# Sparse attention of block 1: the multiply of the probabilities by their reciprocal sums, issued on GpSimd in place of VectorE

## The reference, cut to what matters

```python
y_a = conformer_conv(a_val, a_gate, ...)   # GLU, causal depthwise conv of 31 taps, LayerNorm, swish
y_b = short_gated_conv(b_gate, c_gate, b_h, sc_dw[l])
y_c = dsa_attention(q, k, v, q_idx, k_idx, w_idx)
x = x + jnp.concatenate([y_a, y_b, y_c], axis=-1) @ w_out[l]

# dsa_attention: 8 heads of 64; the top 128 keys of each query by an indexer's score, causal
s = jnp.einsum('bqhd,bqkhd->bqhk', qb, k_sel).astype(jnp.float32) * (dh ** -0.5)
s = jnp.where(jnp.isfinite(top_val)[:, :, None, :], s, -jnp.inf)
p = jax.nn.softmax(s, axis=-1).astype(v.dtype)
return jnp.einsum('bqhk,bqkhd->bqhd', p, v_sel)
```

## Time and profile before

| | |
|---|---|
| median of three runs | 3725.43 us |
| profiled execution | 3722.92 us |
| span of its instructions | 3721.0 us |
| TensorE busy | 97% of the span |
| VectorE busy | 54% |
| ScalarE busy | 33% |
| GpSimd busy | 15% |
| share of TensorE in the chain that ended last | 91% |
| first sparse attention (l = 0) | 550.3 to 612.6 us |
| second (l = 1) | 1741.7 to 1807.4 us |

### The profile page before, as it was taken

The page is one execution under the profiler, slowest core; times in us unless marked ns, Lnnn a source line. Parts: engine busy times, 40 slices in busy tenths (PEclk is TensorE's granted clock), DMA queues, the critical chain, the costliest instruction groups (busy, mean ns, idle before and its releaser), DMA issues.

```text
span 3721.0 us, 45399 instructions
## 1 busy us (share of the span) xinstructions
PE 3624.0 (97%) x15894; PEld 2840.8 (76%) x15894; DVE 2009.4 (54%) x3014; ACT 1210.5 (33%) x1783; POOL 552.4 (15%) x378
## 2 busy tenths in 40 slices
PE   8999998999999999998999999999999999899998
PEld 6887775877887888776687888776688877678887
DVE  5445796555445544679645444635644463564444
ACT  4223354332223222345433322323322232332222
POOL 0000382020002000236203000300300020030002
PEclk9999999999999999999999999999999999999999
DMA  5332331423333333332141333322133332113331
GB/s 149 96 94 80 97 85 41 124 63 94 93 96 91 94 93 96 87 87 68 57 133 53 92 91 96 95 69 63 46 95 92 96 91 80 57 51 96 94 92 62
DMA packets 617232, 318.93 MB, mean 86 GB/s; under 512 B 12144, under 2 KB 615176, under 8 KB 617096
## 3 DMA queue, kind: packets, MB, share of 16 engines
q1 hardware_dynamic: 617096, 317.15, 29.6%
HBM read 314.75 MB, written 2.10 MB: 85 GB/s over the span
## 4 chain that ended last, share of the span: by engine, by line
PE 91%; DVE 4%; ACT 2%; issue 1%; POOL 1%; DMA 0%; POOLq 0%; DVEq 0%; ACTq 0%; SPq 0%
PE bank L443 28%; PE bank L445 28%; PE bank L444 28%; PE bank L537 1%; PE bank L706 1%; PE bank L612 1%; PE bank L690 1%; PE bank L724 1%; PE bank L533 1%; DVE spare L1691 1%; PE bank L732 0%; PE bank L743 0%; DVE u_lo L1182 0%; DVE w_lo L1178 0%; POOL mem L1752 0%
## 5 line engine op out<-in xcount | busy, mean ns | idle before, releaser
L860 ACT ACTIVATE w_hi<-raw 128x1024 fp32r<-128x1024 f32 x602 | 638.1, 1060 | 1854.5 <-PE bank L445 1853.3
L443 PE MATMUL bank<-u_hi,w_hi 128*128 128x512 f32 x3024 | 1220.1, 403 | 2.5 <-DVE u_lo L1182 1.8
L445 PE MATMUL bank<-u_hi,w_lo 128*128 128x512 f32 x3024 | 1197.5, 396 | 0.0
L444 PE MATMUL bank<-u_lo,w_hi 128*128 128x512 f32 x3024 | 1193.6, 395 | 0.0
L1178 DVE TENSOR_TENSOR w_lo<-raw,w_hi 128x1024 fp32r<-128x1024 f32 x602 | 794.9, 1320 | 724.1 <-ACT w_hi L860 723.6
L443 PEld LDWEIGHTS bank<-u_hi,w_hi 128*128 128x128 f32 x3024 | 568.9, 188 | 156.2 <-issue 16.5
L444 PEld LDWEIGHTS bank<-u_lo,w_hi 128*128 128x128 f32 x3024 | 568.9, 188 | 143.4 <-issue 9.3
L445 PEld LDWEIGHTS bank<-u_hi,w_lo 128*128 128x128 f32 x3024 | 568.7, 188 | 139.6
L443 PE MATMUL bank<-h_hi,w_hi 128*128 128x512 f32 (+1 forms) x1696 | 646.2, 381 | 2.1 <-DVE h_lo L1182 2.1
L445 PE MATMUL bank<-h_hi,w_lo 128*128 128x512 f32 (+1 forms) x1696 | 641.6, 378 | 0.0
L444 PE MATMUL bank<-h_lo,w_hi 128*128 128x512 f32 (+1 forms) x1696 | 641.1, 378 | 0.0
(11 more groups left out here) (208 smaller groups left out, 2217.3 us busy)
## 6 DMA issues: line engine op xcount, KB each, us to landing
raw<-in_w_in SPq DMA_DIRECT2D x96, 512.0 KB, 3.8
raw<-in_ffn_w_gate SPq DMA_DIRECT2D x88, 512.0 KB, 3.8
raw<-in_ffn_w_up SPq DMA_DIRECT2D x88, 512.0 KB, 3.8
raw<-in_ffn_w_down SPq DMA_DIRECT2D x64, 512.0 KB, 3.9
raw<-in_w_gate SPq DMA_DIRECT2D x44, 512.0 KB, 3.8
raw<-in_w_up SPq DMA_DIRECT2D x44, 512.0 KB, 3.8
raw<-in_w_out SPq DMA_DIRECT2D x32, 512.0 KB, 4.0
raw<-in_xa_wkv SPq DMA_DIRECT2D x32, 512.0 KB, 3.9
```

The source lines that it names most:

```text
L443: mm(o, w_hi[:, s, w], rhs_hi[:, r], start=k == 0, stop=False)
L444: mm(o, w_hi[:, s, w], rhs_lo[:, r], start=False, stop=False)
L445: ins = mm(o, w_lo[:, s, w], rhs_hi[:, r], start=False, stop=k == kn - 1)
L860: a(w_hi[:, p.slot, :], raw[:, p.slot, :], ACT.Copy).then_inc(rounded, 1)
```

## The change

The reciprocal stays on VectorE, and releases a new semaphore `p_inv`. VectorE no longer waits for it, and goes on. GpSimd waits for `p_inv`, multiplies the two tiles and releases `p_norm`. Its squares for the LayerNorm now stand behind the multiplies of step 4, and its power behind those of step 6.

```diff
@@ block.vector, the sparse attention
                     if 1 <= i < 17:
-                        b, n = (i - 1) % 4, P * ((i - 1) % 4 + 1)
+                        b = (i - 1) % 4
                         v.wait_ge(p_exp, s0 + i)
-                        chain.done(v, nc.vector.reciprocal(small[:, 16 + 2 * b:18 + 2 * b], small[:, 8 + 2 * b:10 + 2 * b]))
-                        for e in range(2):
-                            p_ = pair_s[b][e][:, 0:n]
-                            ins = ts(p_, p_, row_inv[2 * b + e], None, ALU.mult)
-                        ins.then_inc(p_norm, 1)
+                        nc.vector.reciprocal(small[:, 16 + 2 * b:18 + 2 * b], small[:, 8 + 2 * b:10 + 2 * b]).then_inc(p_inv, 1)
@@ block.gpsimd, behind the taps
-                for c in range(2):
-                    pool.wait_ge(ln_cent, 2 * l + c + 1)
-                    tt(y_buf[c], conv[c], conv[c], ALU.mult).then_inc(ln_sq, 1)
-                pool.wait_ge(ln_v, l + 1)
-                tt(ln_inv, ln_var, minus_half[:, 0:NQ], ALU.pow).then_inc(ln_i, 1)
+                for i in range(16):
+                    b, n = i % 4, P * (i % 4 + 1)
+                    pool.wait_ge(p_inv, 16 * l + i + 1)
+                    for e in range(2):
+                        p_ = pair_s[b][e][:, 0:n]
+                        ins = ts(p_, p_, row_inv[2 * b + e], None, ALU.mult)
+                    ins.then_inc(p_norm, 1)
+                    if i == 4:
+                        for c in range(2):
+                            pool.wait_ge(ln_cent, 2 * l + c + 1)
+                            tt(y_buf[c], conv[c], conv[c], ALU.mult).then_inc(ln_sq, 1)
+                    if i == 6:
+                        pool.wait_ge(ln_v, l + 1)
+                        tt(ln_inv, ln_var, minus_half[:, 0:NQ], ALU.pow).then_inc(ln_i, 1)
```

More of the change, by code:

```diff
@@ L325, in two_blocks @@
         masked = sem("masked")
-        s_mm, s_min, p_exp, p_norm, t_mm, t_set, pv_mm = (
-            sem(n) for n in ("s_mm", "s_min", "p_exp", "p_norm", "t_mm", "t_set", "pv_mm"))
+        s_mm, s_min, p_exp, p_inv, p_norm, t_mm, t_set, pv_mm = (
+            sem(n) for n in ("s_mm", "s_min", "p_exp", "p_inv", "p_norm", "t_mm", "t_set", "pv_mm"))
         o_rounded, o_ready = sem("o_rounded"), sem("o_ready")
```

## The result

The changed kernel is slower: 3734.96 us, median of seven runs (3727.38 to 3738.38), against 3722.44 us for the kernel before in seven runs beside it. The ratio is 1.003, with a 95% interval of 1.0019 to 1.0041. That is 12.5 us, above the range of the prediction (3717 to 3730) and on the other side of its forecast. Its profiled execution took 3730.14 us with a span of 3727.9 us.

A forecast was written before the change was run, and what follows sets the result against it. TensorE, busy 97% of the span, was taken as the bound, so only VectorE multiplies it waits for counted. Gains of 1.30 and 0.53 us, 1.83 in each of two attentions, gave 3.7 us: 3721.8 us, range 3717 to 3730.

The forecast's parts named there:

- The price of one multiply: GpSimd's tensor_scalar multiply, absent from the trace, was estimated at 0.71 us for 512 columns.
- The upper end, 1.04: Range end for GpSimd's multiply at 512 columns, from the two-operand multiply; gain 1.11 us a block, 3723.2 us.
- Rival B: GpSimd's multiply costs 1.81 us, like its two-tensor additions; 2.35 us a block slower, 3730.1 us; chance 0.12.
- its line between 1.04 and 1.81 us: Gain or loss by GpSimd's multiply price at 512 columns; the sign turns at about 1.29 us.
- Rival C: TensorE's clock decides in the attentions, falling either way by 3.4 us: 3718.3 or 3725.1 us; chance 0.16.
- The tail: Step 15's multiplies before the last transposes: 1.47 us on GpSimd fits in 2.01; at 1.04 each, 0.12 is lost.
- some 1.4 us nearer to the start of the attention: Centring of the LayerNorm (L1512) on VectorE, expected this much earlier as a sign of being right.
- The first gain is 1.30 us: GpSimd's LayerNorm squares start at 573.26 in place of 574.56, behind the multiplies of step 4.
- TensorE's own work hides it: GpSimd's power behind step 6's pair costs nothing, since its diagonal is wanted only after the value product.
- The lock: Shared ports of VectorE and GpSimd: L1182 waits for GpSimd's multiply until 570.95, a gain of 0.97 instead of 1.41.
- rival D: Lock or GpSimd order takes the 0.97 gain down by 0.71: 3723.2 us, or 3725.4 with L1526's neighbours delayed; chance 0.12.
- small gain of step 9: Step 9's multiplies leave VectorE ahead of L1526, adding 0.53 us, less than ScalarE's wait of 0.76.

The follow-up runs named there:

- e2: Changed kernel with GpSimd's multiply written as a two-tensor form reading the reciprocals as a broadcast: 3719.55 us, 0.9992 of the kernel before.
- e11: Changed kernel with a constant 0.01 in place of the column of reciprocals, leaving out the division by row sums: 3728.75 us, one run.
- e3: Changed kernel with constant matmuls nobody reads ahead of TensorE's waits for the squares and the last multiply: 3722.86 us, 1.0002 of the kernel before.
- e1: Changed kernel without the multiplies, leaving out the division by the row sums: 3717.43 us, 0.9986 of the kernel before.
- e4: Changed kernel with the multiplies of steps 14 and 15 back on VectorE: 3726.29 us, 1.0014 of the kernel before.
- e10: Changed kernel with the multiplies of steps 0 to 4 back on VectorE: 3727.73 us, 1.0022 of the kernel before.
- e7: Changed kernel with e2's form, steps 2, 14 and 15 on VectorE, squares and power moved ahead as in e6: 3716.76 us, 0.9991 of the kernel before.
- e6: Changed kernel with the squares ahead of step 4's multiplies and the power ahead of step 6's: 3726.20 us, 1.0014 of the kernel before.
- e5: Changed kernel with only steps 5 to 13 multiplied on GpSimd, the others back on VectorE: 3719.85 us, 0.9997 of the kernel before.

## Why the prediction was wrong

**The price of one multiply is the step that failed.** "I take 0.71, since the instruction reads one tensor and is of the kind of the 281 ns row" put together the fixed part of one instruction and the slope of another. The fixed part was about right, the slope was not: a memset reads nothing, and its 0.84 ns a column says nothing of an instruction that does; the multiply has 2.5. (The prediction's 0.47 us for 128 columns "by that slope" lies on the line from the 281 ns row to the 1.04 us; the memset's slope would give 0.72. The change's row has 0.63 at 128 columns.) The upper end, 1.04, was taken from the two-operand multiply as if a second tensor could only make it dearer. e2 and e11 show the opposite: the form that reads one tensor and a constant takes 1.55, the one that reads two 1.14.

**Rival B was right in its place and its sign, at 0.12.** But the price alone does not carry the sum: its line between 1.04 and 1.81 us, taken at 1.58, gives +1.3 us a block, 2.6 of the 12.5 in all. By that line the squares come 0.65 us late and the tail loses 1.20 us; the sums of squares came 0.8 and 1.1 us late in the two blocks, and the last wait grew by 1.86 us. What is missing is a queue on GpSimd and the clock.

**The clock was the second step.** Rival C had it as luck, half each way, independent of the rest. But at the two places the waits and the clock go together: behind a wait of 1.4 and 2.6 us for the squares and of 2.2 us for the last pair, both blocks ran the next work at the low clock, and fillers in the same waits took it away there (e3). In the first block 2.7 us of waiting brought 5.6 us of slower work with it. The earlier trace rows held the hint, a value product of 4.10 us at 0.58, and the prediction itself remarked that TensorE "had often idled" before it; it used this for a spread, not for the price of a wait. Rival C is not refuted for the rest of the attention: the value products between the two places fall either way, and in the second block three of them together took 3.2 us less than before the change. The runs of one kernel differ with the clock as well: the 33 runs of the kernel before beside e1 to e4 go from 3716.03 us at a granted 0.985 to 3726.56 at 0.981.

**The tail** had "2.01 us, of which VectorE used 0.88" and asked whether 0.05 + 2 x price fit. It assumed that GpSimd is free when the last reciprocal comes. This row of VectorE over time in the kernel after has that reciprocal:

```profile
608.05 0.17 DVE L1483 RECIPROCAL small<-small 128x2 f32<-128x2 f32 x1 [0.98 <-ACT spare L1012]
```

GpSimd had begun the pair of step 14 at 606.57 and came to the last pair only at 609.38, as GpSimd over time shows:

```profile
609.38 3.10 POOL L1792 TENSOR_SCALAR spare<-spare,small 128x512 f32<-128x512 f32 x2
```

The last reciprocal was done at 608.22, so the last pair stood 1.2 us in a queue before its own 3.1 us. e10 puts the tail at 0.22%, e4 takes it away.

**The front.** The centring "some 1.4 us nearer to the start of the attention" held and more: it starts at 572.01, 21.4 us after the start of the attention against 23.5 before, 2.0 us earlier. "The first gain is 1.30 us" did not: the squares stood behind GpSimd's piece of 6.76 us and started 0.6 us late, the sums of squares 0.8. The prediction let GpSimd begin step 3 as soon as its reciprocal was there. But the pair of step 2, off the chain while VectorE did it, now stood ahead of it in GpSimd's order and ran from 568.69 to about 571.1, while the reciprocal of step 3 was done at 570.28. This is the same queue as in the tail. e1 shows the relief that the argument was about, 1.9 us, and e2 and e7 keep 1.4 to 1.6 of it. "TensorE's own work hides it", of the power, failed in the first block: the power came late at 587.28, and TensorE waited 0.71 us for the diagonal.

**The lock** was to make L1182 wait for GpSimd's multiply. It did not, as VectorE over time in the kernel after shows; GpSimd was multiplying without a break from 568.69 to 575.45:

```profile
570.63 0.69 DVE L1182 SCALAR_TENSOR_TENSOR h_lo<-mem,h_hi 128x512 fp32r<-128x512 f32 x1 [0.35 <-ACT h_hi L1020]
```

In e2, beside the two-tensor form, the same instruction is stretched:

```profile
571.44 1.31 DVE L1182 SCALAR_TENSOR_TENSOR h_lo<-mem,h_hi 128x512 fp32r<-128x512 f32 x1 [0.35 <-ACT h_hi L1020]
```

So the half of rival D that had L1182 wait for whole pairs of multiplies is out: in the change they block it not at all. The other half, the order on GpSimd, was there: the squares waited for three whole pairs, and e6 gets about half of the loss back by the order.

**Right** were the small gain of step 9 (TensorE's wait ahead of its transposes fell from 2.56 to 1.90 us in both blocks) and the reading that only the work ahead of the squares, ahead of L1526 and in the tail counts: e5, which leaves the first and the last alone, changes nothing that can be told.

**What stays open.** The median less the two attentions of the profiled execution is 3591 to 3597 us for all these kernels but e1, where it is 3603.5: its profiled execution, at 3710.41 us, is one of its three fastest, and the attentions of the others may have been longer. Each kernel has one profile, so how much they differ from run to run isn't known, and differences between attentions of single profiles are to be read with that in mind. Why the value products between the two places run slowly in one block and not in another isn't known either. Outside the attentions the profiled executions of the kernels differ by up to 12 us (3585.8 in e10, 3597.9 in e2) without a difference in the work; that wasn't followed up. The cost of the lock by itself wasn't tried.

## What to carry to other kernels

Price an operation that moves to another engine from rows of that very form, and where there are none, measure the form first: two ways to write one multiply differed here by 0.44 us, and that decided whether the move cost 0.3% or nothing. A wait on TensorE can cost more than its length, since the work behind it may run at half the clock; when a kernel gets a new wait like those of 1.3 to 2.6 us here ahead of a stage that ends the chain, reckon it with the slower work behind it, and try constant matmuls in the gap. Ask of every queue whether the engine is free when the operand comes, above all for the last item before the next stage: work that was off the chain on one engine can stand ahead of it on another.

## What the runs showed of the hardware

GpSimd's tensor_scalar on float32 took 0.63 us at 128 columns and 1.58 us at 512, or 1.55 us with a constant. Its tensor_tensor with a broadcast column took 1.14 us in the mean, and 1.02 us in this pair of e2, while VectorE's L1192 was the one that took longer (2.45 us; GpSimd over time):

```profile
584.92 2.04 POOL L1792 TENSOR_TENSOR spare<-spare,small 128x512 f32<-128x512 f32 x2
```

The Trainium skill (GPSIMD Engine Reference, §4.1 "Engine selection") has it the other way round, about half of VectorE's speed for two inputs and "roughly line-rate" for one. Here the measurement decides: VectorE did a pair of tensor_scalars in 0.88 us, GpSimd in 3.16.

The two engines' influence on each other goes by the form, too. The subtraction L1182 with two SBUF inputs took 0.69 us beside GpSimd's tensor_scalar and 1.31 us beside its tensor_tensor, the same in both attentions; the earlier trace rows has 0.68 with GpSimd idle. The Trainium skill (SBUF — State Buffer, "Who interferes with whom") lets it contend with any GpSimd instruction that reads SBUF; the 0.69 us speak against that for tensor_scalar, and the 1.31 us agree for tensor_tensor. VectorE's own tensor_scalar, on the other hand, was slowed by both: the four instructions of the diagonal (L1192), in the kernel before and in the change,

```profile
583.60 0.87 DVE L1192 TENSOR_SCALAR mem<-const,small 128x128 f32<-128x128 f32 x4
```

```profile
588.31 1.66 DVE L1192 TENSOR_SCALAR mem<-const,small 128x128 f32<-128x128 f32 x4 [1.92 <-POOL small L1800]
```

and in e2 they took 2.45 us. Why GpSimd's tensor_scalar is the slower form, and why it leaves L1182 alone, no run here tells.
